# Attention layer of a hybrid decoder trunk: scores and values of two slots in one visit, three such visits per pair of heads

## The chip, the cores and the metric

The kernel runs on one core of a Trainium2 chip. The time is that of the device for one execution of the program, in microseconds (us); before the change its median was 1372.56 us over 3 runs (1372.26 to 1372.92).

## The reference

Four residual layers of 512 tokens and width 1024, each of which is a norm, one combined input projection, a mixer, a gate and an output projection. Layers 0 and 3 are a gated linear recurrence, layer 2 is spatial gating. The change touches only layer 1, dilated attention: 16 heads of 64 columns, three groups of keys with dilation 1, 4 and 16, each with its own q, k, v and softmax. Cut to what matters:

```
proj = rms_norm(x) @ b_w_in                      # q, k, v of 3 groups, and a gate
for g, (window, dilation) in enumerate(((128, 1), (512, 4), (2048, 16))):
    q, k = rms_norm(q_g), rms_norm(k_g)          # per head
    scores = q k^T / 8 - slope * distance        # 128 queries against 2*128 keys (group 0),
    lse = logsumexp(scores)                      # all keys of the residue (groups 1, 2)
    o_g = exp(scores - lse) @ v
w = softmax over the 3 groups of lse
x = x + (sum_g w_g o_g * silu(gate)) @ b_w_out
```

## The kernel before

Each product of the projections is made of three f32r matmuls of 128x512 (high and low halves of both operands), so the weights are split into w_hi by ScalarE (L1231) and w_lo by VectorE (L1730) before TensorE can use them. All f32 work of the attention (scores, transposes, values) is made by plain f32 matmuls between them.

Layer 1 works on a pair of heads at a time. `layer_b` has, for each engine, a body that is run for i = 0 to 8: in body i TensorE projects pair i (`proj`) and mixes pair h = i - 1 (`mix`). Seven bodies do both, the last one (`mix and not proj`) mixes the eighth pair beside the output projection. Where this text numbers pairs, the first is h = 0.

In a body with both, TensorE runs 80 steps `ks` of three dense matmuls: ten banks of eight steps. `steps[ks]` holds what is inserted behind step ks, here called a visit. The dense banks alternate between two accumulators; before a bank is begun again (`bank_free`), ScalarE and VectorE must have taken out the bank before last (`unit`, L1535 and L2143 to L2151, and others).

The softmax of a pair is made in four slots w = 0 to 3. Slots 0 and 1 are group 0 (two token tiles each), slots 2 and 3 are groups 1 and 2. A slot's chain is: `scores(w)` on TensorE (L1010, into the two banks `score`); `bias(w)` (L2182 to L2188) and `peak(w)` (L2196 to L2199) on VectorE, into b_s[w % 2]; `exps(w)` on ScalarE (L1491); `normalise(w)` on VectorE (L2206 to L2215); `turn_p(w)`, the transposes of the probabilities, on TensorE (L1024, into the two banks `turn`); `p_out(w)`, the copies out of them, one half on ScalarE (L1499) and one on VectorE (L2224), into b_pt; `values(w)` on TensorE (L1041, into obank for slots 0 and 1, spare for 2 and 3). Ahead of it stand seven transposes of q, k and v (`turn_qk`, L990, at steps 0 to 3 and 5 to 7) with copies on ScalarE (`qk_out` L1474, `v_out` L1480); behind it `log_sums`, `log_weights`, `turn_lse` (L1053, step 57) and the merge (`dilated_out` L1521, `merge_subtract` L2246, `into_y`).

TensorE takes a slot's scores, the values of two slots before and the transposes of one slot before at one visit: SLOT_AT = (4, 15, 26, 38, 50, 62), thus six visits with score or value matmuls. Score matmuls use half the rows of the array (64x128, the two heads beside each other), value matmuls half of its columns (128x64); transposes and dense matmuls use all of it.

ScalarE and VectorE have a list `plan` of (due time in steps, work), sorted by the due time alone. So the numbers in it give the order of each engine's queue, and no engine looks past the work at its head. Normalisation of slot 0 is due at 10.4, of slot w at SLOT_AT[w] + 8; units at 8.5, 16.5, 24.5 and so on; the splits of weights (`split_lo_chunk`) at 4.7, 10.5, 13.0, 33.0, 33.1, 43.0, 48.0, 53.0, 73.0 and 74.2. In the seventh pair (body i = 7) a square root (ScalarE, 40.1), its inverse (41) and two normalisations of q and k (`norm_qk`, L2167, 41.1) are in the queues besides.

In the last body the order is written by hand for every engine. TensorE fills the gaps with the output projection: `first_half(k)` is six dense matmuls with block k of the branch's output and needs its low half, `split_y(k)` of VectorE (L1788); `second_half(k)` is six more, into the banks `score`, and needs all four biases done. The end of the layer is the last block: values(3), merge, split of block 7, and `output_projection`.

Of the kernel before, what the change touches and what calls it, by code (L numbers as in the profile page):

```python
# [22 lines left out]
P = 128  # L23
# [45 lines left out]
B_SLOTS = 4  # L69
SLOT_AT = (4, 15, 26, 38, 50, 62)  # L70

# [71 lines left out]
def build(nc, x, norm_w, a_w_in, a_lower_bounds, a_o_norm_w, a_w_out, b_w_in, b_q_norm_w, b_k_norm_w,  # L143
# [10 lines left out]
    with ctx:  # L154
# [66 lines left out]
        b_w, b_t = b_wt[:, 0], b_wt[:, 1]  # L221
        b_pt, at = carve(at, 2, S)
        b_raw, at = carve(at, 3 * TT, 256)
        b_v, at = carve(at, 2, 2 * TT, P)
# [36 lines left out]
        obank = ps[6]  # L261
        spare = ps[7]


# [335 lines left out]
        def _(pe):  # L600
# [370 lines left out]
            def layer_b(n):  # L971
                def body(j, par, proj, mix, end):
# [20 lines left out]
                    def scores(w):  # L993
                        stream = w // 2
                        if w % 2 == 0:
                            pe.wait_ge(qkT_done, h * B_TURNS + (6 if stream else 2))
                        if w or later:
                            pe.wait_ge(s_biased, h * B_SLOTS + w)
                        for k in range(2):
                            u = 2 * w + k  # L1000
                            t = u % TT
                            tile = slice(t * P, (t + 1) * P)
                            for g in (1, 2) if stream else (0,):
                                for e in range(2):
                                    head = slice(e * 64, e * 64 + 64)
                                    if stream:
                                        to, keys = slice((g - 1) * P, g * P), tile
                                    else:
                                        to, keys = slice(keys_from(u), 2 * P), slice(max(t - 1, 0) * P, (t + 1) * P)
                                    last = nc.tensor.matmul(slot_half(score[e], k)[:, to], b_qk[head, 2 * g, tile],  # L1010
                                                            b_qk[head, 2 * g + 1, keys], start=True, stop=True)
                                    if k == 1 and g != 1:
                                        last.then_inc(s_ready, 1)

                    def turn_p(w):
                        pe.wait_ge(p_done, h * B_SLOTS + (w + 1))
                        for e in range(2):
                            if w == 0:
                                pe.wait_ge(qkT_done, h * B_TURNS + B_TURNS)
                            else:  # L1020
                                pe.wait_ge((pT_act, pT_dve)[e], h * B_SLOTS + w)
                            for at in range(keys_from(w), 4 * P, P):
                                k, key = divmod(at, 2 * P)
                                last = nc.tensor.transpose(turn[e][:, at:at + P], b_s[w % 2][:, k, e, key:key + P], ident[:])  # L1024
                            last.then_inc(pT_ready, 1)

                    def values(w):
                        stream = w // 2
                        pe.wait_ge(pT_act, h * B_SLOTS + (w + 1))
                        pe.wait_ge(pT_dve, h * B_SLOTS + (w + 1))  # L1030
                        if w % 2 == 0 and later:
                            pe.wait_ge((mg_sub, t_copied)[stream], h)
                        if w == 0:
                            pe.wait_ge(qkT_done, h * B_TURNS + B_TURNS)
                        for at in range(keys_from(w), 4 * P, P):
                            k, c = divmod(at // P, 2)
                            t = 2 * (w % 2) + k
                            v = b_v[:, prev, c * TT + t] if stream else b_v0[:, t - 1 + c]
                            for e in range(2):
                                head = slice(e * 64, e * 64 + 64)  # L1040
                                last = nc.tensor.matmul((obank, spare)[stream][head, t * P:(t + 1) * P], v[:, head],  # L1041
                                                        b_pt[:, e, at:at + P], start=(c == 0 or at == keys_from(w)),
                                                        stop=(c == 1))
                        last.then_inc(bo_ready, 1)
# [34 lines left out]
                    if mix and not proj:  # L1079
                        scores(0)  # L1080
                        turn_qk(2)
                        turn_qk(3)
                        first_half(0)
                        turn_qk(4)
                        scores(1)
                        turn_qk(5)
# [5 lines left out]
                        first_half(4)  # L1092
                        turn_p(1)
                        values(0)
                        scores(3)
                        first_half(5)
                        values(1)
                        turn_p(2)
                        second_half(0)
                        values(2)  # L1100
                        first_half(6)
                        second_half(1)
                        turn_p(3)
                        second_half(2, 3)
                        turn_lse()
                        values(3)
                        second_half(4, 5, 6)
# [3 lines left out]
                    if mix:  # L1111
                        for b in range(B_TURNS):
                            steps.setdefault(QK_TURNS[b], []).append(lambda b=b: turn_qk(b))
                        for s in range(B_SLOTS + 2):
                            at = steps.setdefault(SLOT_AT[s], [])
                            if s < B_SLOTS:
                                at.append(lambda w=s: scores(w))
                            if s >= 2:
                                at.append(lambda w=s - 2: values(w))
                            if 1 <= s <= B_SLOTS:  # L1120
                                at.append(lambda w=s - 1: turn_p(w))
                        steps[57] = [turn_lse]
# [105 lines left out]
        def _(act):  # L1228
# [224 lines left out]
            def layer_b(n):  # L1453
                B0, per = ACC0[n], len(B_PARTS)

                def body(j, par, proj, mix, end):
# [5 lines left out]
                    def qk_out(b, h=h, later=later):  # L1462

                        act.wait_ge(qkT_ready, h * B_TURNS + (b + 1))
                        if later:
                            act.wait_ge(s_ready, h * 8)
                        g, part = divmod(b, 2)
                        col = 18 + 3 * part + g
# [25 lines left out]
                    def p_out(w):  # L1494
                        act.wait_ge(pT_ready, h * 8 + (2 * w + 1))
                        if w or later:
                            act.wait_ge(bo_ready, h * B_SLOTS + w)
                        first = keys_from(w)
                        nc.scalar.activation(b_pt[:, 0, first:], turn[0][:, first:], ACT.Copy).then_inc(pT_act, 1)  # L1499

# [130 lines left out]
                    if mix:  # L1631
                        for b in range(B_TURNS):
                            plan.append((QK_TURNS[b] + 1, v_out if b == 6 else lambda b=b: qk_out(b)))
                        for w in range(B_SLOTS):
                            plan.append((SLOT_AT[w] + 4.5, lambda w=w: exps(w, (0, 1))))
                            plan.append((SLOT_AT[w + 1] + 0.8, lambda w=w: p_out(w)))
                        plan.append((46, log_sums))
# [89 lines left out]
        def _(dve):  # L1727
# [398 lines left out]
            def layer_b(n):  # L2126
# [3 lines left out]
                def body(j, par, proj, mix, end):  # L2130
# [38 lines left out]
                    def bias(w):  # L2169
# [4 lines left out]
                        for e in range(2):  # L2174
                            dve.wait_ge(s_ready, h * 8 + (2 * w + e + 1))
                            for g in (1, 2) if stream else (0,):
                                to = slice((g - 1) * P, g * P) if stream else slice(0, 2 * P)
                                dist = b_dist[:, 2 * P * stream:][:, to]
                                ratio = slope[:, bass.ds(h * 2 + (16 * g + e), 1)]
                                of = score[e][:].rearrange("p (k c) -> p k c", k=2)  # L2180
                                if w == 0:
# [37 lines left out]
                    def p_out(w):  # L2219
                        dve.wait_ge(pT_ready, h * 8 + (2 * w + 2))  # L2220
                        if w or later:
                            dve.wait_ge(bo_ready, h * B_SLOTS + w)
                        first = keys_from(w)
                        nc.vector.tensor_copy(b_pt[:, 1, first:], turn[1][:, first:]).then_inc(pT_dve, 1)  # L2224

# [36 lines left out]
                    if mix and not proj:  # L2262
# [8 lines left out]
                        normalise(1)  # L2271
                        bias(2)
                        peak(2)
                        split_y(n, 5)
                        p_out(1)
                        bias(3)
                        normalise(2)
                        peak(3)
                        p_out(2)
                        split_y(n, 6)  # L2280
                        split_lo_out(n, 4)
# [33 lines left out]
                    if mix:  # L2315
                        for w in range(B_SLOTS):
                            plan.append((SLOT_AT[w] + 0.5, lambda w=w: bias(w)))
                            plan.append((SLOT_AT[w] + 0.6, lambda w=w: peak(w)))
                            plan.append((SLOT_AT[w] + (6.4 if w == 0 else 8), lambda w=w: normalise(w)))
                            plan.append((SLOT_AT[w + 1] + 0.9, lambda w=w: p_out(w)))  # L2320
                        plan.append((46.2, log_weights))
# [159 lines left out]
```

## Time and profile before

| what | value |
|---|---|
| median of 3 runs | 1372.56 us |
| profiled execution, its own time | 1372.53 us |
| its span | 1370.7 us |
| TensorE busy | 1361.8 us (99%) |
| VectorE busy | 940.0 us (69%) |
| ScalarE busy | 695.6 us (51%) |
| layer 1, mixing part | about 343 to 880 us of the span |

The page shows one execution. PE is TensorE, DVE VectorE, ACT ScalarE. Matmuls overlap one another, so TensorE's durations are longer than the distances of their starts, and the starts are what is to be read; an f32 matmul of the program is shown as two instructions. A row of the timeline joins neighbours of one line on one engine; in brackets stands the idle time of the engine ahead of it and what ended it.

### The profile page before, as it was taken

What the parts mean: (1) busy time and instruction counts of PE and PEld (TensorE: products, weight loads), DVE (VectorE), ACT (ScalarE), POOL (GpSimd) and SP (SyncE); (2) the same over time, 40 slices, a digit from 0 to 9 for tenths busy, and PEclk for the clock granted to TensorE, in tenths of its full rate; (3) what the DMA queues carried; (4) which work ended last, traced back from release to release, by engine and by line L of the source; (5) the groups of instructions that cost most, each with busy time, mean ns of one, the idle gap of its engine ahead of it and who ended that gap; (6) DMA issues with size and microseconds to landing.
All of it is one profiled execution on the core that took longest, in us unless ns stands there. A gap on an engine that the chain in (4) does not pass through costs nothing.

```text
span 1370.7 us, 22566 instructions
## 1 busy us (share of the span) xinstructions
PE 1361.8 (99%) x8951; PEld 1125.1 (82%) x8951; DVE 940.0 (69%) x1651; ACT 695.6 (51%) x1243; POOL 92.4 (7%) x128
## 2 busy tenths in 40 slices
PE   9999999999999999999999999999999999999999
PEld 8888887888887878788878787799888888888877
DVE  7677779663666676667666676767657567777882
ACT  6444545353646465656565566553434344555460
POOL 2111212000000000000000000000000011211110
PEclk9999999999999999999999999999999999999999
DMA  6322233422222222222222122323333322232321
GB/s 190 93 78 77 63 90 96 116 78 83 71 78 78 77 77 77 78 77 77 77 76 79 56 68 63 111 61 93 93 92 93 108 78 78 62 93 68 89 61 62
DMA packets 211691, 113.66 MB, mean 83 GB/s; under 512 B 3743, under 2 KB 209889, under 8 KB 211586
## 3 DMA queue, kind: packets, MB, share of 16 engines
q1 hardware_dynamic: 211202, 112.02, 28.5%
q8 instruction: 72, 1.18, 0.4%
q14 instruction: 33, 0.27, 0.1%
q0 software_dynamic: 384, 0.20, 0.1%
HBM read 110.10 MB, written 2.10 MB: 82 GB/s over the span
## 4 chain that ended last, share of the span: by engine, by line
PE 94%; DVE 3%; ACT 2%; issue 1%; DMA 0%; SPq 0%; ACTq 0%; DVEq 0%
PE ps L606 38%; PE ps L621 37%; PE scores L621 4%; PE scores L1010 2%; PE ps L1041 2%; PE ps L1024 2%; PE ps L990 2%; PE ps L841 1%; PE scores L812 1%; PE ps L843 1%; PE ps L635 1%; PE scores L830 1%; DVE w_lo L1730 1%; PE scores L799 1%; PE scores L778 1%
## 5 line engine op out<-in xcount | busy, mean ns | idle before, releaser
L606 PE MATMUL ps<-op_hi,w_hi 128*128 128x512 f32 (+1 forms) x800 | 318.0, 397 | 0.1
L606 PE MATMUL ps<-op_lo,w_hi 128*128 128x512 f32 (+1 forms) x800 | 305.7, 382 | 0.0
L606 PE MATMUL ps<-op_hi,w_lo 128*128 128x512 f32 (+1 forms) x800 | 304.8, 381 | 0.0
L621 PE MATMUL ps<-w_hi,op_hi 128*128 128x512 f32 (+1 forms) x760 | 299.3, 394 | 3.5 <-DVE op_lo L1788 1.8
L621 PE MATMUL ps<-w_lo,op_hi 128*128 128x512 f32 (+1 forms) x760 | 288.4, 379 | 0.0
L621 PE MATMUL ps<-w_hi,op_lo 128*128 128x512 f32 (+1 forms) x760 | 287.6, 378 | 0.0
L1730 DVE TENSOR_TENSOR w_lo<-raw,w_hi 128x1024 fp32r<-128x1024 f32 x200 | 240.5, 1227 | 36.3 <-ACT w_hi L1231 35.7
L1231 ACT ACTIVATE w_hi<-raw 128x1024 fp32r<-128x1024 f32 x200 | 202.7, 1051 | 19.3 <-PE ps L621 11.2
L606 PEld LDWEIGHTS ps<-op_lo,w_hi 128*128 128x128 f32 x800 | 150.4, 188 | 30.6
L606 PEld LDWEIGHTS ps<-op_hi,w_hi 128*128 128x128 f32 x800 | 150.6, 188 | 27.3 <-issue 0.4
L606 PEld LDWEIGHTS ps<-op_hi,w_lo 128*128 128x128 f32 x800 | 150.9, 189 | 24.8
L621 PEld LDWEIGHTS ps<-w_hi,op_hi 128*128 128x128 f32 x760 | 143.1, 188 | 33.5 <-issue 6.7
L581 POOL TENSOR_TENSOR scratch<-scratch 128x256 f32<-128x256 f32 x112 | 85.9, 767 | 1234.3 <-DVE scratch L1903 942.6
L621 PEld LDWEIGHTS ps<-w_lo,op_hi 128*128 128x128 f32 x760 | 143.0, 188 | 27.9
L621 PEld LDWEIGHTS ps<-w_hi,op_lo 128*128 128x128 f32 x760 | 143.4, 189 | 23.0 <-issue 0.2
L1918 DVE TENSOR_TENSOR scratch<-scratch 128x256 f32<-128x256 f32 x112 | 72.1, 644 | 23.0 <-PE scores L812 12.1
L1491 ACT ACTIVATE scratch<-scratch 128x256 f32<-128x256 f32 (+1 forms) x128 | 61.7, 484 | 21.3 <-DVE scratch L2199 21.1
L1499 ACT ACTIVATE scratch<-ps 128x512 f32<-128x512 f32 (+1 forms) x32 | 18.3, 571 | 78.1 <-PE ps L1024 76.2
L1371 ACT ACTIVATE scratch<-scratch 32x128 f32<-32x128 f32 x64 | 19.7, 308 | 60.3 <-DVE scratch L1981 59.8
L1474 ACT ACTIVATE scratch<-ps,vec 128x512 f32<-128x512 f32 x48 | 39.3, 854 | 17.7 <-PE ps L990 16.8
L2188 DVE SCALAR_TENSOR_TENSOR scratch<-scratch,slope,scores 128x256 f32<-128x256 f32 (+1 forms) x80 | 37.7, 530 | 12.1 <-PE scores L1010 12.1
L1795 DVE TENSOR_TENSOR xt<-xt,ps 128x512 f32<-128x512 f32 (+1 forms) x27 | 17.7, 666 | 39.5 <-PE ps L621 39.5
(217 smaller groups left out, 1810.6 us busy)
## 6 DMA issues: line engine op xcount, KB each, us to landing
raw<-in_b_w_in SPq DMA_DIRECT2D x80, 512.0 KB, 4.0
raw<-in_a_w_in SPq DMA_DIRECT2D x64, 512.0 KB, 4.3
raw<-in_c_w_in SPq DMA_DIRECT2D x24, 512.0 KB, 4.3
raw<-in_a_w_out SPq DMA_DIRECT2D x16, 512.0 KB, 4.5
raw<-in_b_w_out SPq DMA_DIRECT2D x8, 512.0 KB, 4.0
raw<-in_c_w_out SPq DMA_DIRECT2D x8, 512.0 KB, 4.9
xt<-in_x SPq DMA_DIRECT2D x4, 512.0 KB, 6.5
y<-in_norm_w SPq DMA_DIRECT2D x3, 512.0 KB, 4.9
```

What stands on the lines that cost most here:

```text
L581: nc.gpsimd.tensor_tensor(k, k, decay.unsqueeze(2).to_broadcast([P, nb, m]), ALU.mult).then_inc(keys_moved, 1)
L606: last = nc.tensor.matmul(bank, a, b, start=(k == 0 and p == 0), stop=(k == KT - 1 and p == 2))
L621: last = nc.tensor.matmul(bank, a, b, start=(k == 0 and p == 0), stop=(k == KT - 1 and p == 2))
L990: last = nc.tensor.transpose(turn[b % 2][:, t * P:(t + 1) * P], of, ident[:])
L1010: last = nc.tensor.matmul(slot_half(score[e], k)[:, to], b_qk[head, 2 * g, tile], b_qk[head, 2 * g + 1, keys], start=True, stop=True)
L1024: last = nc.tensor.transpose(turn[e][:, at:at + P], b_s[w % 2][:, k, e, key:key + P], ident[:])
L1231: nc.scalar.activation(w_hi[:, ring], raw[:, slot], ACT.Copy).then_inc(hi_done, 1)
L1474: nc.scalar.activation(to, of, ACT.Copy, scale=vec[:, col:col + 1]).then_inc(qkT_done, 1)
L1491: nc.scalar.activation(p, p, ACT.Exp, bias=b_m[:, 2 * u + e:2 * u + e + 1], accum_out=b_l[:, 2 * u + e:2 * u + e + 1]).then_inc(e_done, 1)
L1730: nc.vector.tensor_tensor(w_lo[:, ring], raw[:, slot], w_hi[:, ring].bitcast(F32), ALU.subtract).then_inc(lo_done, 1)
L1918: nc.vector.tensor_tensor(q, q, decay.unsqueeze(2).to_broadcast([P, nb, m]), ALU.mult).then_inc(queries_moved, 1)
L2188: last = nc.vector.scalar_tensor_tensor(to_s[:, :, e, to], dist, ratio, of[:, :, to], ALU.mult, ALU.add)
```

## The change

SLOT_AT goes; each kind of step has its own due times. Scores of slots 0 and 1 are made at step 4, those of slots 2 and 3 at step 28, followed by the values of slots 0 and 1; the values of slots 2 and 3 are made at step 53. Transposes stand alone at 15, 25, 41 and 49. The scores of slot 1 go to the banks obank and spare, those of slot 3 to the banks turn (`slot_banks`), and the transposed probabilities of slots 1 and 3 go to b_qk[:, 0:2] (`b_p`), the q and k of group 0. On VectorE, bias and peak of slots 2 and 3 stand behind one another (28.5 to 28.8), ahead of unit 3 (32.5). In the last body the orders by hand change as the diff shows.

```diff
 B_SLOTS = 4
-SLOT_AT = (4, 15, 26, 38, 50, 62)
+SCORES_AT = (4, 28)
+BIAS_AT = (4.5, 14.5, 28.5, 28.7)
+EXPS_AT = (8.5, 18.5, 31.9, 36)
+NORMAL_AT = (10.4, 22.1, 36.1, 44.1)
+TURN_AT = (15, 25, 41, 49)
+VALUES_AT = (28, 53)

...
         b_pt, at = carve(at, 2, S)
+        b_p = (b_pt, b_qk[:, 0:2], b_pt, b_qk[:, 0:2])
         b_raw, at = carve(at, 3 * TT, 256)
...
         spare = ps[7]
+        slot_banks = (score, (obank, spare), score, turn)

...
                 pe.wait_ge(qkT_done, h * B_TURNS + (6 if stream else 2))
-            if w or later:
-                pe.wait_ge(s_biased, h * B_SLOTS + w)
+            if w == 0 and later:
+                pe.wait_ge(s_biased, h * B_SLOTS - 1)
+            if w == 1 and later:
+                pe.wait_ge(mg_sub, h)
+                pe.wait_ge(t_copied, h)
+            if w == 2:
+                pe.wait_ge(s_biased, h * B_SLOTS + 1)
+            if w == 3:
+                pe.wait_ge(pT_act, h * B_SLOTS + 2)
+                pe.wait_ge(pT_dve, h * B_SLOTS + 2)
             for k in range(2):
...
                             to, keys = slice(keys_from(u), 2 * P), slice(max(t - 1, 0) * P, (t + 1) * P)
-                        last = nc.tensor.matmul(slot_half(score[e], k)[:, to], b_qk[head, 2 * g, tile],
+                        last = nc.tensor.matmul(slot_half(slot_banks[w][e], k)[:, to], b_qk[head, 2 * g, tile],
                                                 b_qk[head, 2 * g + 1, keys], start=True, stop=True)
...
             pe.wait_ge(p_done, h * B_SLOTS + (w + 1))
+            if w == 2:
+                pe.wait_ge(s_biased, h * B_SLOTS + B_SLOTS)
             for e in range(2):
...
             pe.wait_ge(pT_dve, h * B_SLOTS + (w + 1))
-            if w % 2 == 0 and later:
-                pe.wait_ge((mg_sub, t_copied)[stream], h)
             if w == 0:
+                pe.wait_ge(s_biased, h * B_SLOTS + 2)
                 pe.wait_ge(qkT_done, h * B_TURNS + B_TURNS)
...
                     last = nc.tensor.matmul((obank, spare)[stream][head, t * P:(t + 1) * P], v[:, head],
-                                            b_pt[:, e, at:at + P], start=(c == 0 or at == keys_from(w)),
+                                            b_p[w][:, e, at:at + P], start=(c == 0 or at == keys_from(w)),
                                             stop=(c == 1))
...
             scores(0)
+            scores(1)
             turn_qk(2)
...
             turn_qk(4)
-            scores(1)
             turn_qk(5)
...
             turn_p(1)
+            first_half(5)
+            scores(3)
             values(0)
-            scores(3)
-            first_half(5)
             values(1)
+            second_half(0)
             turn_p(2)
-            second_half(0)
-            values(2)
             first_half(6)
...
             turn_lse()
+            values(2)
             values(3)
...
                 steps.setdefault(QK_TURNS[b], []).append(lambda b=b: turn_qk(b))
-            for s in range(B_SLOTS + 2):
-                at = steps.setdefault(SLOT_AT[s], [])
-                if s < B_SLOTS:
-                    at.append(lambda w=s: scores(w))
-                if s >= 2:
-                    at.append(lambda w=s - 2: values(w))
-                if 1 <= s <= B_SLOTS:
-                    at.append(lambda w=s - 1: turn_p(w))
+            for w in range(B_SLOTS):
+                steps.setdefault(SCORES_AT[w // 2], []).append(lambda w=w: scores(w))
+            for w in range(B_SLOTS):
+                steps.setdefault(VALUES_AT[w // 2], []).append(lambda w=w: values(w))
+                steps.setdefault(TURN_AT[w], []).append(lambda w=w: turn_p(w))
             steps[57] = [turn_lse]
...
                 act.wait_ge(s_ready, h * 8)
+                if b < 2:
+                    act.wait_ge(bo_ready, h * B_SLOTS)
             g, part = divmod(b, 2)
...
             act.wait_ge(pT_ready, h * 8 + (2 * w + 1))
-            if w or later:
-                act.wait_ge(bo_ready, h * B_SLOTS + w)
+            if w > 1 or w == 0 and later:
+                act.wait_ge(bo_ready, h * B_SLOTS + w - 1)
             first = keys_from(w)
-            nc.scalar.activation(b_pt[:, 0, first:], turn[0][:, first:], ACT.Copy).then_inc(pT_act, 1)
+            nc.scalar.activation(b_p[w][:, 0, first:], turn[0][:, first:], ACT.Copy).then_inc(pT_act, 1)

...
             for w in range(B_SLOTS):
-                plan.append((SLOT_AT[w] + 4.5, lambda w=w: exps(w, (0, 1))))
-                plan.append((SLOT_AT[w + 1] + 0.8, lambda w=w: p_out(w)))
+                plan.append((EXPS_AT[w], lambda w=w: exps(w, (0, 1))))
+                plan.append((TURN_AT[w] + 0.8, lambda w=w: p_out(w)))
             plan.append((46, log_sums))
...
                     ratio = slope[:, bass.ds(h * 2 + (16 * g + e), 1)]
-                    of = score[e][:].rearrange("p (k c) -> p k c", k=2)
+                    of = slot_banks[w][e][:].rearrange("p (k c) -> p k c", k=2)
                     if w == 0:
...
             dve.wait_ge(pT_ready, h * 8 + (2 * w + 2))
-            if w or later:
-                dve.wait_ge(bo_ready, h * B_SLOTS + w)
+            if w > 1 or w == 0 and later:
+                dve.wait_ge(bo_ready, h * B_SLOTS + w - 1)
             first = keys_from(w)
-            nc.vector.tensor_copy(b_pt[:, 1, first:], turn[1][:, first:]).then_inc(pT_dve, 1)
+            nc.vector.tensor_copy(b_p[w][:, 1, first:], turn[1][:, first:]).then_inc(pT_dve, 1)

...
             bias(2)
+            p_out(1)
             peak(2)
             split_y(n, 5)
-            p_out(1)
             bias(3)
...
             peak(3)
+            split_y(n, 6)
             p_out(2)
-            split_y(n, 6)
             split_lo_out(n, 4)
...
             for w in range(B_SLOTS):
-                plan.append((SLOT_AT[w] + 0.5, lambda w=w: bias(w)))
-                plan.append((SLOT_AT[w] + 0.6, lambda w=w: peak(w)))
-                plan.append((SLOT_AT[w] + (6.4 if w == 0 else 8), lambda w=w: normalise(w)))
-                plan.append((SLOT_AT[w + 1] + 0.9, lambda w=w: p_out(w)))
+                plan.append((BIAS_AT[w], lambda w=w: bias(w)))
+                plan.append((BIAS_AT[w] + 0.1, lambda w=w: peak(w)))
+                plan.append((NORMAL_AT[w], lambda w=w: normalise(w)))
+                plan.append((TURN_AT[w] + 0.9, lambda w=w: p_out(w)))
             plan.append((46.2, log_weights))
...
```

## Rows read from the trace of the kernel before

**Rows 1.** The page: busy time and instructions of each engine, granted TensorE clock by slice.
```profile
PE 1361.8 (99%) x8951; PEld 1125.1 (82%) x8951; DVE 940.0 (69%) x1651; ACT 695.6 (51%) x1243; POOL 92.4 (7%) x128
...
PEclk9999999999999999999999999999999999999999
```
**Rows 2.** TensorE's waits, whole run: line, releaser, us in total, times, longest.
```profile
PE ps L621 <- DVE op_lo L1788: 1.8, 4, 1.2
...
PE ps L1024 <- DVE scratch L2215: 0.8, 1, 0.8
...
PE ps L621 <- DVE scratch L2154: 0.4, 1, 0.4
```
**Rows 3.** Timeline of TensorE, steady pair, step 4: start, duration, line, operation, count.
```profile
490.09 0.40 PE L621 MATMUL ps<-w_lo,op_hi 128*128 128x512 f32 x1
490.42 0.93 PE L1010 MATMUL scores<-scratch 64*128 64x128 f32 x8
...
491.61 0.40 PE L621 MATMUL ps<-w_hi,op_lo 128*128 128x512 f32 x1
```
**Rows 4.** The same timeline at step 15.
```profile
500.35 1.14 PE L1010 MATMUL scores<-scratch 64*128 64x256 f32 x8
...
502.36 0.39 PE L621 MATMUL ps<-w_hi,op_lo 128*128 128x512 f32 x1
```
**Rows 5.** The same timeline at step 26.
```profile
509.75 1.16 PE L1010 MATMUL scores<-scratch 64*128 64x128 f32 x16
510.84 0.88 PE L1041 MATMUL ps<-scratch 128*64 128x128 f32 x12
511.65 1.09 PE L1024 MATMUL ps<-ident,scratch 128*128 128x128 f32 x8
...
512.81 0.39 PE L621 MATMUL ps<-w_hi,op_lo 128*128 128x512 f32 x1
```
**Rows 6.** The same timeline at step 62.
```profile
543.38 1.09 PE L1041 MATMUL ps<-scratch 128*64 128x128 f32 x16
544.40 0.50 PE L621 MATMUL ps<-w_hi,op_hi 128*128 128x512 f32 x1
544.74 0.40 PE L621 MATMUL ps<-w_hi,op_lo 128*128 128x512 f32 x1
```
**Rows 7.** Timeline of ScalarE in the same pair, exponentials of slot 0.
```profile
495.66 1.28 ACT L1491 ACT_TABLE_LOAD   x1
```
**Rows 8.** Timeline of VectorE in the same pair; in brackets idle time and its releaser.
```profile
498.85 0.18 DVE L2206 RECIPROCAL scratch<-scratch 128x4 f32<-128x4 f32 x1 [2.38 <-ACT scratch L1491]
...
499.40 0.69 DVE L2211 TENSOR_TENSOR scratch<-scratch 128x512 f32<-128x512 f32 x1
...
505.91 0.68 DVE L2151 TENSOR_REDUCE scratch<-scratch 128x8 f32<-128x512 f32 x1
...
507.29 1.22 DVE L2215 TENSOR_TENSOR scratch<-scratch 128x1024 f32<-128x1024 f32 x1
```
**Rows 9.** Timeline of VectorE in the seventh pair.
```profile
812.39 2.36 DVE L2167 TENSOR_TENSOR scratch<-scratch 128x1024 f32<-128x1024 f32 x2
...
816.56 1.22 DVE L2215 TENSOR_TENSOR scratch<-scratch 128x1024 f32<-128x1024 f32 x1
```
**Rows 10.** Timeline of VectorE in the last pair.
```profile
855.97 1.65 DVE L2188 SCALAR_TENSOR_TENSOR scratch<-scratch,slope,scores 128x256 f32<-128x256 f32 x4
...
858.79 0.68 DVE L1788 TENSOR_TENSOR op_lo<-y,op_hi 128x512 fp32r<-128x512 f32 x1
859.39 0.68 DVE L2224 COPY scratch<-ps 128x512 f32<-128x512 f32 x1
```
**Rows 11.** Timeline of TensorE in the last pair.
```profile
856.34 1.03 PE L1024 MATMUL ps<-ident,scratch 128*128 128x128 f32 x8
...
859.53 0.50 PE L621 MATMUL ps<-w_hi,op_hi 128*128 128x512 f32 x1 [0.26 <-DVE op_lo L1788]
...
873.95 1.09 PE L1041 MATMUL ps<-scratch 128*64 128x128 f32 x16
```

## The prediction

> **What bounds the kernel now.** I read the page first: TensorE is busy in 1361.8 of 1370.7 us [rows 1]. Then who TensorE waits for: the entries that touch the attention layer are the low half of a branch output, 1.8 us in four times, a normalisation, 0.8 us once, and a reduction of an accumulator, 0.4 us once [rows 2]. So nearly every microsecond is TensorE's own queue, and the question is what the inserted visits cost it. Third, TensorE's timeline of one steady pair (485 to 556 us) shows that a "busy" engine still loses time at its changes of kind. Dense matmuls start 0.227 us apart (three make a step, 0.68). From a dense matmul to the first score matmul it is 0.33 us [rows 3]. The visits' prices follow by start times: from the dense matmul before a visit to the second one after it, less two intervals (0.45). Last, the timelines of ScalarE and VectorE in the same pair give the chain that hands the probabilities back [rows 7, 8].
>
> The profiled execution took 1372.53 us, the median of the runs is 1372.56, so the sum made on the one stands for the other.
>
> **Visits before.** Slot 0 alone at step 4: 491.61-490.09-0.45 = 1.07 [rows 3]. Step 15, eight score instructions and six transposes: 502.36-500.35+0.32-0.45 = 1.88 [rows 4]. Step 26, 16 score, 12 value, 8 transpose instructions: 512.81-509.75+0.32-0.45 = 2.93 [rows 5]. Step 38 has four more value instructions, and 16 of them take 1.02 where 12 take 0.81 [rows 5, 6]: 3.14. Step 50, values and eight transposes: 0.32+1.02+(512.81-511.65)-0.45 = 2.05. Step 62, values alone: 544.74-543.38+0.32-0.45 = 1.23 [rows 6]. Together 12.30 us.
>
> **Visits after.** An f32 matmul is two instructions and the two heads run side by side, so 16 score instructions are eight start times, 0.11 apart; of the 1.09 they take, 0.2 is the slow first and last interval. Adding slot 1 to step 4 costs four start times of double width, 0.86: 1.93. Eight transposes behind tile matmuls take 512.81-511.65 = 1.16 to the second dense matmul, 0.06 of it a slow first interval; behind dense ones they cost 0.23+1.16-0.06-0.45 = 0.88 [rows 5], 0.11 each and nothing for entry, so those at steps 15, 25, 41 and 49 cost 0.66, 0.88, 0.88, 0.88. Step 28: 0.32 entry, 1.09+0.89 for two slots of scores, 0.81+0.87 for two of values, 0.34 to the second dense matmul, less 0.45: 3.87. Step 53: 1.23+0.87 = 2.10. Together 11.20. TensorE's own work is shorter by 1.10 us a pair, 7.7 over the seven pairs that run beside projections.
>
> **What eats it in the steady pair.** Visit 4 is now 0.86 longer, so the transposes at steps 5, 6 and 7 come 0.86 later. ScalarE's exponentials of slot 0 stand in its queue behind the copy-out of step 7; their table load began at 495.66 and VectorE waited 2.38 us for them until 498.85 [rows 7, 8]. From there VectorE has no idle time until the next exponentials: reciprocal and scaling, two weight splits, bias and peak of slot 1, copy, unit 1, end at 506.59; normalisation of slot 1 ends at 508.51 [rows 8]. No order in that stretch is changed, so the whole chain moves with step 7: 507.45 and 509.37.
> TensorE meanwhile is early: visit 15 lost 1.22 and visit 4 gained 0.86, net 0.35. Step 24 needs unit 1 out of its bank; it stood at 509.75-0.32-8x0.227 = 507.61 [rows 5] and would now stand at 507.26, but the bank is free at 507.5: 0.25 lost. The transposes of slot 1 follow step 25; without waits they would start at 509.75-0.09-0.68-0.35 = 508.63, and the normalisation is there at 509.44 with some 0.07 for the signal: 0.81 lost in all, the first 0.25 included, and 0.06 for a slow first interval. Before, they came at 511.65, with three microseconds to spare [rows 5]. The transposes of slot 0 just fit (501.12 against 500.09+0.86+0.07 = 501.02). So a steady pair keeps 1.10-0.87 = 0.22.
> The new queue order behind step 28 hides: bias, peak, bias, peak, unit 3, two splits and the normalisation of slot 2 take 1.3+1.66+1.2+1.6+1.2+1.2+2.3+1.4 = 11.9 us from the visit's start, and its transposes come 3.87+0.06+13x0.68 = 12.8 after it. Steps 40 and 53 keep over half a microsecond the same way. Scores of slot 3 wait for the copies of slot 1, done 2 us before. Scores of slot 1 now use the output banks and wait for the merge of the pair before, which ended some ten microseconds earlier. Six such pairs: -1.3 us.
>
> **The seventh pair** has two query/key normalisations in VectorE's queue at 41.1 (812.39, 2.36 us) and ended the normalisation of slot 3 at 817.78, when its transposes were already due [rows 9]. The transposes move from behind the value matmuls of step 50 to step 49, 0.09+1.02+0.68 earlier: due 815.9. VectorE can gain only the 1.0 that step 39 comes sooner: 813.7, then copy 0.6, split 1.1, normalisation 1.4 make 816.8. About 1.0 is lost there, in place of 0.1 before. The 0.4 us for the reduction of unit 4, which now runs earlier in the queue, goes [rows 2]. With the 0.22 of the other pairs this one comes out 1.0-0.1-0.35-0.2, say 0.4 slower.
>
> **The last pair** runs beside the output projection, with orders written by hand, and here the change costs most. Before, slot 1's transposes (856.34) were followed by values(0) and scores(3), and first_half(5) began at 859.53, 0.26 late on the low half of output block 5; VectorE had run bias, peak (1.17 between them), split_y(5), then the copy [rows 10, 11]. Now first_half(5) stands directly behind the transposes, ready at 857.2. And VectorE runs the copy before the peak: bias until 857.6, copy 0.6, peak 1.15, split_y(5) 0.68 end at 860.1. TensorE idles 3.0 us and begins 0.6 later than before, with scores(3) and values(0) still ahead of it (1.8). Then bias(3) waits for scores(3): 862.9 to 864.6, normalisation until 865.9, peak 867.1, split_y(6) 867.65; exponentials (498.85-495.66 less the table load of 1.28, some 2.0) and normalisation of slot 3 end at 871.3. TensorE waits 0.25 for the bias, 0.7 for split_y(6), 0.85 for the last normalisation, 1.8 in place of 0.85 [rows 2]. Merged visits give back 0.5. Values(3) ends +0.6+1.8+0.95-0.5 = 2.85 later than at 873.95+1.02 [rows 11], and merge, split and the last projection hang on it as before.
> What the idle gap itself may cost: the granted clock is at its upper level, 2.4 GHz, in all slices, but the longest wait among these is 1.2 us [rows 1, 2]; nothing shows whether 3.0 us is borne. The Trainium skill (TensorE: Matmul & The Clock Gate, "Part 1: The HAM clock gate") says an array left idle long enough is gated to half its clock until it has been busy again. By that rule the stretch behind the gap would be slower; it is a rival below, no term of the sum.
>
> **Sum.** 1372.5 - 1.3 + 0.4 + 2.85 = 1374.5 us.
>
> **Rivals.**
> A (0.60), as summed. Its own range, with 0.2 either way per steady pair and 1 on the last: 1372.3 to 1376.7.
> B, steady stalls are smaller or hidden: if the slot-0 chain doesn't hang on step 7 (ScalarE free earlier), all 7.7 count: 1372.5-7.7+2.85 = 1367.7; half of it, 1371. For it: VectorE is idle 2.38 us just before. Against: the table load follows the copy-out without a gap. 0.12 (half of it below 1369.8).
> C, the last pair isn't held, because its wait for split_y(5) ends sooner than my queue says: 1372.5-1.3+0.4 = 1371.6. Against: the rows of both engines leave no idle time to take it from. 0.10.
> D, slower: the 3.0 us gap brings TensorE to 1.2 GHz. The work of the six microseconds behind it (scores, values, six and six dense) at half speed is up to 6 more, part of it inside later waits: about 3.5, 1378. It decides from the gap's length alone. 0.08.
> E, slower: the tile visits don't get cheaper when merged (the loss belongs to each matmul). Then 1.10 is not saved; of the stalls 0.34 goes, since TensorE is less early: each pair 0.5 slower, 1372.5+3.5+0.4+3.3 = 1379.7. Against: the visit of eight score instructions cost 1.07 [rows 3], as much as sixteen take by themselves [rows 5], so a good part is fixed. 0.04.
> F, the steady pair gains nothing, because chain and TensorE meet worse (another 0.3 at the transposes of slots 2 or 3): 1376.5. 0.06.
>
> **Numbers.** 0.2% (2.7 us) is about what a measurement of this kernel tells from no change: below 1369.8 is faster, above 1375.3 slower. Faster: half of B and a little of C, 0.08. Slower: D, E, F (0.18), and of A the upper quarter, 0.15: 0.33. Same: 0.59. Range 1370.5 to 1377.3.
>
> **What would show it.** In the profile after: TensorE waits for the normalisation (now L2230 or so) once in each steady pair, 0.5 to 0.6 us, and for unit 1's reduction 0.2; the visit at step 28 has 32 score and 28 value instructions in 3.7 us; steady pairs start 0.2 us closer together; in the last pair one wait of 3 us for split_y(5) at about 857 less what the pairs saved. Wrong if that wait is missing, if the pairs are a full 1.1 us closer, or if the granted clock falls behind it.

## The result, and the profile after

The changed kernel takes 1375.01 us (median of 22 runs, 1372.87 to 1376.21), the one before 1372.51 (22 runs, 1371.7 to 1372.92): 1.0018 of it, 95% interval 1.0012 to 1.0025. It is slower by 2.5 us, less than the 0.2% taken as no change, and 0.5 above the forecast. The page of its profiled execution (1374.76 us, span 1373.0):

```profile
PE 1358.5 (99%) x8951; PEld 1127.2 (82%) x8951; DVE 937.7 (68%) x1651; ACT 693.1 (50%) x1242; POOL 92.5 (7%) x128
```

TensorE has as many instructions as before, is busy 3.3 us less [rows 1] and ends 2.3 later. Who it waits for (line, releaser, total us, times, longest), against [rows 2]:

```profile
PE ps L628 <- DVE op_lo L1803: 4.9, 5, 2.8
PE ps L1041 <- DVE scratch L2230: 2.6, 8, 1.0
PE ps L628 <- DVE scratch L2166: 1.3, 7, 0.2
```

Unit 1's reduction (L2166) now holds it seven times, once in each pair that runs beside a projection; the normalisation (L2230, before L2215) holds it eight times, once in each of those pairs and once more in the seventh; and one wait of 2.8 us for a split of the output blocks has appeared. Where each part of the layer begins, from TensorE's timeline (first transposes of the second, third, seventh and last pair, first transposes of layer 2's input), before and after:

```profile
414.59 0.66 PE L990 MATMUL ps<-ident,scratch 128*128 128x128 f32 x4
485.73 0.66 PE L990 MATMUL ps<-ident,scratch 128*128 128x128 f32 x4
...
770.19 0.66 PE L990 MATMUL ps<-ident,scratch 128*128 128x128 f32 x4
...
837.97 0.60 PE L990 MATMUL ps<-ident,scratch 128*128 128x128 f32 x4
...
894.57 1.03 PE L635 MATMUL ps<-ident,y 128*128 128x128 f32 x8
```

```profile
414.31 0.66 PE L997 MATMUL ps<-ident,scratch 128*128 128x128 f32 x4
485.13 0.66 PE L997 MATMUL ps<-ident,scratch 128*128 128x128 f32 x4
...
768.45 0.66 PE L997 MATMUL ps<-ident,scratch 128*128 128x128 f32 x4
...
836.35 0.60 PE L997 MATMUL ps<-ident,scratch 128*128 128x128 f32 x4
...
896.85 1.03 PE L642 MATMUL ps<-ident,y 128*128 128x128 f32 x8
```

A steady pair takes 70.82 in place of 71.14 us, the seventh 67.90 in place of 67.78, and the last body with the end of the layer 60.50 in place of 56.60. So the steady pairs gain 1.7 together and the last body loses 3.9: the whole result.

**The steady pair.** TensorE at step 28 (before [rows 5]), then around steps 24 and 25:

```profile
440.76 0.39 PE L628 MATMUL ps<-w_lo,op_hi 128*128 128x512 f32 x1
441.08 1.16 PE L1025 MATMUL scores<-scratch 64*128 64x128 f32 x16
442.08 1.06 PE L1025 MATMUL ps<-scratch 64*128 64x128 f32 x16
443.07 1.75 PE L1057 MATMUL ps<-scratch 128*64 128x128 f32 x28
...
445.08 0.40 PE L628 MATMUL ps<-w_hi,op_lo 128*128 128x512 f32 x1
```

```profile
435.56 0.39 PE L628 MATMUL ps<-w_lo,op_hi 128*128 128x512 f32 x1
436.16 0.47 PE L628 MATMUL ps<-w_hi,op_hi 128*128 128x512 f32 x1 [0.21 <-DVE scratch L2166]
...
437.38 0.39 PE L628 MATMUL ps<-w_lo,op_hi 128*128 128x512 f32 x1
438.00 1.09 PE L1041 MATMUL ps<-ident,scratch 128*128 128x128 f32 x8 [0.24 <-DVE scratch L2230]
```

The merged visit costs 445.08-440.76-0.45 = 3.87, to the hundredth what the rows of before gave. But the matmuls at 436.16 and 438.00 start 0.60 and 0.62 behind their neighbours, where 0.23 is the rule: 0.37 and 0.39 lost. (The bracket counts idle time only from the modelled end of the matmul before, so it shows 0.2; starts tell the loss.) VectorE in the same stretch, against [rows 8]:

```profile
428.27 0.18 DVE L2221 RECIPROCAL scratch<-scratch 128x4 f32<-128x4 f32 x1 [2.38 <-ACT scratch L1506]
...
435.34 0.67 DVE L2166 TENSOR_REDUCE scratch<-scratch 128x8 f32<-128x512 f32 x1
...
436.72 1.23 DVE L2230 TENSOR_TENSOR scratch<-scratch 128x1024 f32<-128x1024 f32 x1
```

From the reciprocal to the end of the normalisation it takes 9.68 us, 9.66 before: the chain is the same, and comes later. It begins 428.27-414.31 = 13.96 us behind the first transposes of the pair, before 498.85-485.73 = 13.12: 0.84 later, where the prediction had 0.86.

**The last body**, TensorE, then VectorE, against [rows 10, 11]:

```profile
854.51 1.09 PE L1041 MATMUL ps<-ident,scratch 128*128 128x128 f32 x8
858.40 0.69 PE L628 MATMUL ps<-w_hi,op_hi 128*128 128x512 f32 x1 [2.80 <-DVE op_lo L1803]
858.90 0.63 PE L628 MATMUL ps<-w_hi,op_lo 128*128 128x512 f32 x1
859.32 0.63 PE L628 MATMUL ps<-w_lo,op_hi 128*128 128x512 f32 x1
...
861.16 1.52 PE L1025 MATMUL ps<-scratch 64*128 64x128 f32 x16
```

```profile
855.94 0.69 DVE L2239 COPY scratch<-ps 128x512 f32<-128x512 f32 x1
856.54 1.21 DVE L2214 TENSOR_REDUCE scratch<-scratch 128x4 f32<-128x1024 f32 x1
857.67 0.68 DVE L1803 TENSOR_TENSOR op_lo<-y,op_hi 128x512 fp32r<-128x512 f32 x1
862.79 1.66 DVE L2203 SCALAR_TENSOR_TENSOR scratch<-scratch,slope,ps 128x256 f32<-128x256 f32 x4 [4.44 <-PE ps L1025]
```

The copy, the peak, split_y(5): TensorE stands until 858.40, and the bias of slot 3 after it until 862.79. Before the gap a dense matmul is shown with 0.39 us and the next starts 0.23 later; behind it with 0.63, and the next starts 0.43 later. (The 0.69 of the first one is no measure: the first behind a gap is longer at full clock too, 0.50 in experiment 2.) Three stretches, each with from:to, length, busy time and count of TensorE, of its weight loads, of VectorE, ScalarE and GpSimd, then the granted clock as a share of 2.4 GHz, the share of the DMA engines and GB/s:

```profile
856.00:858.00 2.00, 0.00 (x0) 0.00 (x0) 2.00 (x4) 0.21 (x1) 0.00 (x0) 1.00 0.01 4
858.50:861.90 3.40, 3.40 (x12) 2.36 (x14) 0.00 (x0) 1.88 (x7) 0.00 (x0) 0.51 0.00 0
862.00:865.00 3.00, 2.86 (x42) 2.46 (x41) 2.18 (x6) 0.00 (x0) 0.00 (x0) 1.00 0.00 0
```

The next dense matmul could have started 0.85 us behind the transposes (as 815.36 to 816.21 in the seventh pair), at 855.36; it starts at 858.40. That is a gap of 3.0 us by the starts; the row shows 2.8, counted from a modelled end. From 858.5 to 861.9 TensorE was granted 1.2 GHz, then 2.4 again.

### The profile page after: what moved, and what is told of

Its sections match the earlier page's. It is cut to its first block, busy times and chain, and to the rows that moved or that the text cites. A ratio compares the mean times of both kernels' runs of the same rounds, so it can differ in the third digit from the quotient of the medians.

```text
span 1373.0 us, 22565 instructions
## 1 busy us (share of the span) xinstructions
PE 1358.5 (99%) x8951; PEld 1127.2 (82%) x8951; DVE 937.7 (68%) x1651; ACT 693.1 (50%) x1242; POOL 92.5 (7%) x128
## 3 DMA queue, kind: packets, MB, share of 16 engines
q8 instruction: 72, 1.18, 0.4%
## 4 chain that ended last, share of the span: by engine, by line
PE 87%; DVE 7%; ACT 4%; issue 1%; DMA 0%; SPq 0%; ACTq 0%; DVEq 0%
PE ps L613 38%; PE ps L628 31%; PE scores L628 4%; ACT scratch L1506 2%; PE ps L1057 2%; DVE w_lo L1745 2%; PE ps L1041 1%; PE ps L997 1%; PE ps L848 1%; PE ps L1025 1%; PE scores L1025 1%; PE scores L819 1%; DVE scratch L2203 1%; DVE scratch L2214 1%; PE ps L642 1%
## 5 line engine op out<-in xcount | busy, mean ns | idle before, releaser
L2161 DVE COPY scratch<-ps 128x256 f32<-128x256 f32 x32 | 13.5, 422 | 67.1 <-ACT scratch L1556 67.1
L1552 ACT ACTIVATE scratch<-ps 128x256 f32<-128x256 f32 x32 | 12.2, 381 | 92.7 <-PE ps L628 92.7
```

## Experiments

Each was compared with the kernel before on the same chip: it took 1372.54 us (33 runs) beside experiments 1 to 4 and 1372.65 (27 runs) beside 5 to 8, 1372.51 in the section above. The changed kernel was not run again beside them; its 1375.01 is that of the section above, and differences to it rest on these three medians being 0.14 us apart. "The queue theory" is that of the prediction, with the half clock added.

**1. The last body as before, the steady pairs changed.**

In short, not line by line:

```diff
-slot_banks[w], b_p[w], the new waits and orders in every body
+if proj (bodies 0 to 7): those; last body: banks, waits and orders of before
```

> The changed kernel with the last body (eighth pair beside the output projection) in its banks, waits and orders of before; the seven steady pairs keep the change. Queue theory (the steady pairs gain 0.3 us each but the seventh, and all of the loss is made in the last body): the last body takes what it took before, so the time is 1372.5 less the 1.6 us by which the last body now starts earlier, 1370.9 (ratio to before 0.9988), and no spell of half clock. Rival (the loss belongs to the new steady pairs, for instance through the shared banks carried into the last body): not below 1372.5.

Measured 1370.97 us (0.9990, 0.9981 to 0.9998), the granted clock full throughout. The layer's end from the last pair's start takes 892.57-835.98 = 56.59 us, as before. The loss sits in the last body alone; without it the change is a gain of 1.6.

**2. The gap filled.**

```diff
 turn_p(1)
+for _ in range(24):
+    nc.tensor.transpose(obank[:, 0:P], ident[:], ident[:])
 first_half(5)
```

> The changed kernel with 24 transposes of a constant into a free bank placed in the last body behind the transposes of slot 1, where TensorE otherwise idles for 3 us; they take 24 x 0.109 = 2.6 us, less than the wait. Clock theory (the gap alone costs nothing more, but the spell of 3.4 us at half clock behind it costs 1.7 to 2): granted clock full all through, 1373.0 to 1373.3. Rival (the loss is the waits alone and the slow spell is swallowed by the later waits): unchanged at 1375.0.

Measured 1373.33 us (1372.92 to 1373.69), 1.0007 of the kernel before (0.9998 to 1.0016), and the mean granted clock is 1.000 in all 11 runs. TensorE's timeline:

```profile
855.28 2.78 PE L1112 MATMUL ps<-ident 128*128 128x128 f32 x24
858.24 0.50 PE L628 MATMUL ps<-w_hi,op_hi 128*128 128x512 f32 x1 [0.18 <-DVE op_lo L1806]
...
895.15 1.03 PE L642 MATMUL ps<-ident,y 128*128 128x128 f32 x8
```

first_half(5) starts as late as before the filling (3.9 us behind the transposes of slot 1, which begin at 854.35), yet the body takes 895.15-836.19 = 58.96 us and not 60.50. So of its 3.9 us, 2.4 are waits and 1.5 the half clock. Work that computes nothing makes the kernel 1.7 us faster (1375.01 less 1373.33).

**3. Transposes of slot 1 at step 27.**

```diff
-TURN_AT = (15, 25, 41, 49)
+TURN_AT = (15, 27, 41, 49)
```

> The changed kernel with the transposes of slot 1 at step 27 in place of 25. Queue theory: in each of the seven steady pairs TensorE no longer stands before the normalisation of slot 1 (0.4 us idle and 0.06 of slow start), while the wait for unit 1 before step 24 stays; pairs 70.4 us apart in place of 70.8, 1375.0 - 7 x 0.45 = 1371.9. Rival (the wait only moves, to the scores of slot 3, which need the copies of these transposes, now two steps later): pairs stay at 70.8 and the time at 1375.0.

Measured 1371.85 us (0.9992, 0.9983 to 1.0001); pairs 483.74-413.33 = 70.41 apart. TensorE's waits:

```profile
PE ps L628 <- DVE scratch L2166: 1.3, 7, 0.2
...
PE ps L1041 <- DVE scratch L2230: 1.0, 1, 1.0
```

The wait for the normalisation is left only in the seventh pair, the one for unit 1 stays. Its runs fall in two groups, four at 1369.74 to 1369.90 and seven at 1371.67 to 1373.00. The profiled one is of the lower group:

```profile
852.00:855.00 3.00, 0.20 (x3) 0.08 (x1) 2.87 (x5) 1.02 (x4) 0.00 (x0) 1.00 0.01 3
855.00:858.00 3.00, 3.00 (x30) 2.33 (x32) 0.23 (x1) 1.90 (x7) 0.00 (x0) 1.00 0.00 0
```

The same gap stands at 852 to 855 (2.80 us by the row again), and the clock behind it is full. The last body takes 891.82-832.86 = 58.96 us, as long as in experiment 2, here with no filling. The mean granted clock of the whole execution is 1.000 in the four lower runs and 0.999 or 0.998 in the seven others. So the same program on the same chip either pays about two microseconds for the gap or doesn't. The changed kernel agrees: its two runs with a mean clock of 1.000 took 1372.87 and 1373.19, the other 20, with 0.999 or 0.998, at least 1374.5.

**4. A weight split behind unit 1.**

```diff
-(5, 10.5), (6, 13.0), (7, 33.0)
+(5, 10.5), (6, 17.0), (7, 33.0)
```

> The changed kernel with VectorE's weight split due at 13.0 moved behind unit 1 (due 17.0), nothing else. Queue theory: bias, peak, copy and unit 1 come 1.14 us sooner, so the wait before step 24 goes, and the normalisation of slot 1 comes 0.5 sooner, since VectorE had 0.5 us idle ahead of it; the wait at step 25 shrinks to 0.3 or less. Pairs 70.3 us apart, 1371.5. Rival (TensorE waits for something that moves with its own step 7 and not for VectorE's queue): pairs stay at 70.8, 1375.0.

Measured 1370.58 us (0.9987, 0.9978 to 0.9996); pairs 483.44-413.21 = 70.23 apart. Neither wait is left in a steady pair:

```profile
PE ps L628 <- DVE op_lo L1803: 4.9, 5, 2.8
...
PE ps L1041 <- DVE scratch L2230: 1.0, 1, 1.0
```

It is 0.9 us below the forecast; 0.6 of that is the pairs, each faster by 0.59 and not 0.5. To change the order of VectorE's queue was enough to take both waits away. In the changed kernel it had no idle time from the reciprocal up to unit 1, and 0.49 us ahead of the normalisation (for ScalarE's exponentials of slot 1, which come behind the peak); but it had work there that nobody was waiting for. The mean clock is 0.999 in all 11 runs, and in the profiled one the half clock stands behind the gap.

**5. Scores of slot 1 in a visit of their own at step 8.**

```diff
-steps.setdefault(SCORES_AT[w // 2], []).append(lambda w=w: scores(w))
+steps.setdefault(8 if w == 1 else SCORES_AT[w // 2], []).append(lambda w=w: scores(w))
```

> The changed kernel with the scores of slot 1 in a visit of their own at step 8, behind the last transposes of q, k and v, in place of step 4. Queue theory (the steady waits come from the 0.86 us by which visit 4 delays the transposes at 5 to 7 and with them the exponentials of slot 0): that chain comes 0.86 sooner and TensorE waits neither before step 24 nor at 25; the visit apart costs 0.36 more for a second entry and exit. Pairs 71.13 - 1.10 + 0.36 = 70.4 us apart, in place of 70.8, and 1375.0 - 3 = 1372.0. Rival (the chain is bound by VectorE's own work and not by step 7): the waits stay and the extra visit is paid besides, pairs 71.2.

Measured 1371.65 us (0.9990, 0.9982 to 0.9999), again in two groups (four runs at 1369.48 to 1369.72 with a mean clock of 1.000, the others from 1371.51 with 0.999 or 0.998). Pairs 484.21-413.83 = 70.38 apart, both steady waits gone. This is the sharpest test of the chain: one visit more for TensorE, 0.4 dearer, and the pair is faster by as much, because visit 4 no longer holds back the transposes at 5 to 7.

**6. The seventh pair's normalisations later.**

```diff
-plan.append((41, lambda: invert(0, slice(0, 32))))
-plan.append((41.1, lambda: norm_qk((0, 1))))
+plan.append((54.4, lambda: invert(0, slice(0, 32))))
+plan.append((54.5, lambda: norm_qk((0, 1))))
```

> The changed kernel with the inverse and the two normalisations of q and k in the seventh pair due at 54.4 and 54.5 in VectorE's queue in place of 41. Queue theory: the wait of 1.0 us before the transposes of slot 3 in that pair goes, it takes 66.9 us in place of 67.9, everything else as it was: 1374.0. Rival (the copies of slot 3 or unit 4, which follow in the same queue, take its place): 67.9 and 1375.0.

That pair takes 834.95-768.27 = 66.68 in place of 67.90 us: a little more than expected. The time is 1372.92 us (1.0003, 0.9994 to 1.0011), 2.1 below the changed kernel where the pair explains 1.2. The profiled execution, with the half clock in it, took 1373.40, 1.36 below the changed kernel's: the two profiles differ by little more than the pair explains. Over the 11 runs the mean clock is 1.000 in five (1372.46 to 1372.64) and 0.999 in six (1372.92 to 1373.40). It fell less often than in the changed kernel, which goes the right way; but the two groups lie closer together than those of experiment 3, and how much of the other 0.9 this is stays open.

**7. TensorE's order in the last body alone.**

```diff
 turn_p(1)
-first_half(5)
-scores(3)
 values(0)
+scores(3)
+first_half(5)
 values(1)
-second_half(0)
 turn_p(2)
+second_half(0)
```

> The changed kernel, banks and queues of ScalarE and VectorE kept, with only TensorE's order in the last body altered: behind the transposes of slot 1 come values(0), scores(3), first_half(5), values(1), transposes of slot 2, second_half(0). Order theory (not the banks but first_half(5) standing first holds TensorE and, through scores(3), the third bias): scores(3) wait 0.5 us for the copies of slot 1, first_half(5) 0.6 for its split, the long wait and the half clock are gone, the last body takes within 0.2 us of what it took before, 1370.9. Rival (the shared banks hold it: scores(3) cannot start before the copies out of its banks are done, and all that follows is late anyway): 1.5 us or more of the loss stays, 1372.5 or above.

Measured 1370.21 us (0.9982, 0.9974 to 0.9991), 0.7 better than expected:

```profile
854.19 1.09 PE L1041 MATMUL ps<-ident,scratch 128*128 128x128 f32 x8
855.21 0.88 PE L1057 MATMUL ps<-scratch 128*64 128x128 f32 x12
856.45 1.16 PE L1025 MATMUL ps<-scratch 64*128 64x128 f32 x16 [0.36 <-DVE scratch L2239]
858.08 0.50 PE L628 MATMUL ps<-w_hi,op_hi 128*128 128x512 f32 x1 [0.47 <-DVE op_lo L1803]
```

The same wait for split_y(5) ends at the same point, but values and scores stand ahead of it and only 0.36 and 0.47 us are idle; the body takes 892.16-836.02 = 56.14 us. Banks and the other queues are the changed kernel's: it was the order of TensorE's own queue. Two steps were moved at once, first_half(5) behind values and scores, and the transposes of slot 2 ahead of second_half(0). The rows show the first of these end the long wait; what the second adds was not tried alone.

**8. Together: step 27, the split, the normalisations, the order of experiment 7.**

> The changed kernel with transposes of slot 1 at step 27, the weight split behind unit 1, the two normalisations of the seventh pair at 54.5 and TensorE's order in the last body of e7. If the waits were all that hid the gain, TensorE's own saving of 1.10 us shows whole: steady pairs 70.0 us apart (71.13 before), the seventh 66.0, the last body as before; 1372.5 - 6 x 1.13 - 1.8 = 1363.9, ratio 0.9937. Rival (other waits come up once these are gone, at steps 40, 53 or 57): 1366 or above.

Measured 1363.41 us (5 runs, 1362.69 to 1363.77), 0.9934 of the kernel before (0.9921 to 0.9948). Pairs 482.86-412.90 = 69.96 apart, 1.18 less than before, the seventh 828.54-762.73 = 65.81, the last body 884.72-828.54 = 56.18. Of TensorE's waits for the normalisation this is left:

```profile
PE ps L1041 <- DVE scratch L2230: 0.3, 1, 0.3
```

It stands in the last body; no wait is left in a pair beside a projection. Six steady pairs make 7.1 of the nine microseconds, the seventh 2.0, the last body 0.4. The 7.1 belong to the change: the kernel before had no such wait in a steady pair that these moves could have taken away. In the seventh pair and the last body it had (0.4 and 0.8 us, [rows 2]), and the same moves were not tried on it, so there the share of the change isn't shown.

## Why the prediction was right, and where it was not

- Visits: TensorE's saving of 1.10 us a pair was right, a little small. Nothing but the waits hid it, since 1.18 shows in experiment 8; and a visit apart costs 0.4 (experiment 5, 0.36 by the rows), so rival E is out.
- The steady waits: 0.87 predicted; measured 70.82-69.96 = 0.86 against experiment 8, of which 0.37 and 0.39 show at the two places named. I had divided them 0.25 and 0.6: the wait for unit 1 ends 436.16-436.01 = 0.15 us after the reduction, and I had let it end 0.05 after. The cause (the chain rides on the transposes of step 7) is shown by experiments 4 and 5, which take away the waits by moving VectorE's work and TensorE's visit. Six pairs gave -1.66 in place of -1.3. Rivals B and F are out. (B's "half of it" is 1371.5 by its own terms, not 1371.)
- The seventh pair: +0.12 in place of +0.4; the wait itself was nearly as forecast (815.36-814.02-0.23 = 1.1 us late, 1.0 forecast) and experiment 6 takes it away. The part that it shares with the other pairs was 0.3 and not 0.2; the rest of the difference isn't explained:

```profile
814.02 0.39 PE L628 MATMUL ps<-w_lo,op_hi 128*128 128x512 f32 x1
815.36 1.09 PE L1041 MATMUL ps<-ident,scratch 128*128 128x128 f32 x8 [0.96 <-DVE scratch L2230]
816.21 0.47 PE L628 MATMUL ps<-w_hi,op_hi 128*128 128x512 f32 x1
```

- The last body: the gap was 3.0 us at the place named, ended by the row named, and rival C is out. At full clock it lost 58.96-56.60 = 2.36 and not 2.85. The term that was mis-sized is the wait for the last normalisation: I had 0.85, and in experiment 3, whose last body is the changed kernel's at full clock, it is 865.71-865.18-0.23 = 0.30. TensorE, then VectorE's peak and ScalarE ahead of it:

```profile
865.18 0.39 PE L628 MATMUL scores<-w_lo,op_hi 128*128 128x512 f32 x1
865.71 1.09 PE L1041 MATMUL ps<-ident,scratch 128*128 128x128 f32 x8
```

```profile
860.70 1.21 DVE L2214 TENSOR_REDUCE scratch<-scratch 128x4 f32<-128x1024 f32 x1
```

```profile
861.62 0.60 ACT L1514 ACTIVATE scratch<-ps 128x512 f32<-128x512 f32 x1 [4.72 <-PE ps L1041]
862.11 0.50 ACT L1506 ACTIVATE scratch<-scratch 128x256 f32<-128x256 f32 x1
```

The peak ends at 861.91 and the exponentials start at 862.11, 0.2 behind it. My figures (peak 867.1, normalisation's end 871.3, less 2.0 for the exponentials and 1.4 for the normalisation) leave 0.8 there, which is the 0.55 too much. ScalarE's copy of its half of the transposes of slot 2 stands ahead of the exponentials and starts at 861.62, before all eight transposes are shown done (862.08): it waits for its own half only.

- The clock: this is the step that failed. The sum had the half clock at nothing, and rival D's mechanism, given 0.08, came: 1.2 GHz in the profiled execution, and a mean clock under 1.000 in 20 of 22 runs. It cost 1.5 us by the last body (60.50 against 58.96) and about 2 between the groups of runs, not 3.5. One of the prediction's own signs of being wrong, that the granted clock falls behind the wait, has come. D is not right as it stands either: it let the gap's length alone decide, and in experiment 3 the same gap was followed by a full clock in four runs of eleven. By the Trainium skill's rule (TensorE: Matmul & The Clock Gate, "Part 1: The HAM clock gate") this was to be reckoned with: an array left idle long enough drops to half its clock until it has been busy again. The profiled execution agrees, with 1.2 GHz for 3.4 us behind the gap; the rule as the prediction told it doesn't say why some runs were spared.

So the waits and the saving were foreseen, but that the time came out within 0.5 us was luck, two errors of opposite sign. The three terms of the sum were together 1.1 us too dear (1.95 forecast, -1.66+0.12+2.36 = 0.82 measured): at full clock the kernel takes 1372.87 and 1373.19 in its two such runs, 1373.33 with the gap filled. The half clock of nearly every run put 1.5 to 2 back.

## What to carry to other kernels

When work is merged on the busiest engine, price two things apart: what the engine saves, and what now stands ahead of whichever short operation begins another engine's chain. Here 0.86 us ahead of three transposes ate 0.86 of 1.18 saved. An engine with next to no idle time can still be late for no good reason: look for work in its queue that no one needs yet, and move that. In a hand-written order look at the step with the latest input: here other ready work in front of it hid most of 3 us of waiting, and an idle gap of the matrix engine can be charged again through its clock.

## What the hardware showed that I had not expected

An idle gap of 3.0 us on TensorE (2.8 by the row) was followed by 1.2 GHz in some executions and by 2.4 in others of the same program. The profiles show where the clock fell; of the other runs only the mean clock is known. It is under 1.000 in 20 of 22 runs of the changed kernel, in seven of eleven of experiments 3 and 5, and in all eleven of experiment 4, with the same gap in all their profiles. In experiment 3 the two groups lie 2 us apart. In the four profiles that show a spell at 1.2 GHz (changed kernel, experiments 4 to 6) it is 3.4 us long each time, but it doesn't start with the work: 0.27 us ahead of the first matmul behind the gap in experiment 5 (854.95 against 855.22), 0.04 behind it in experiment 4, 0.14 in the changed kernel, 0.55 in experiment 6. Four runs of the changed kernel have a mean of 0.998 and are among its seven slowest (1375.25 to 1376.21); by an estimate from that mean (over 0.0015 of 1373 us, twice) they spent more than 4.1 us at half clock, and no profile shows one of those. What decides wasn't found. With 24 transposes of a constant in the gap the clock stayed up: 2.4 GHz around it in the profiled execution, a mean of 1.000 in all 11 runs, which lay within 0.8 us. Waits of up to 1.2 us elsewhere in these profiles never lowered it.
